# One reciprocal moved ahead of a minimum: sink attention on one Trainium2 core

## What is computed

```python
scores = jnp.einsum('bnqkgd,bnskd->bnkgqs', qb, kb).astype(jnp.float32) * (HEAD_DIM ** -0.5)
...
scores = jnp.where(valid[None, :, None, None], scores, NEG_INF)
sink = sinks.astype(jnp.float32).reshape(N_KV_HEADS, GQA_GROUP)[None, None, :, :, None, None]
sink = jnp.broadcast_to(sink, scores.shape[:-1] + (1,))
probs = jax.nn.softmax(jnp.concatenate([scores, sink], axis=-1), axis=-1)[..., :-1]
out = jnp.einsum('bnkgqs,bnskd->bnqkgd', probs.astype(v.dtype), vb)
```

## Time and profile before

| | |
|---|---|
| median of 3 runs | 1983.57 us (1983.26 to 1983.79) |
| the profiled execution | 1982.3 us |
| its span | 1980.5 us |
| mean granted TensorE clock | 0.996 |
| attention stage, first to last normalisation | 1004.4 to 1111.5 us of the span |

### The profile page before, as it was taken

The page is one execution under the profiler, slowest core; times in us unless marked ns, Lnnn a source line. Parts: engine busy times, 40 slices in busy tenths (PEclk is TensorE's granted clock), DMA queues, the critical chain, the costliest instruction groups (busy, mean ns, idle before and its releaser), DMA issues.

```text
span 1980.5 us, 28829 instructions
## 1 busy us (share of the span) xinstructions
PE 1929.2 (97%) x9242; PEld 1583.7 (80%) x9242; DVE 1431.4 (72%) x2388; ACT 910.5 (46%) x1738; POOL 464.0 (23%) x464
## 2 busy tenths in 40 slices
PE   7899999999999999999999999999999999999998
PEld 7778888888888878888866687788888888888787
DVE  6987777777777786576578748777777777777863
ACT  5654344444444453343268645444444344444531
POOL 3311222222212221010036211222122221212310
PEclk9899999999999999999999999999999999999999
DMA  5333322233333350231000113233332323335201
GB/s 210 107 96 96 95 90 87 79 99 94 102 92 93 109 183 14 67 112 54 0 12 2 59 48 112 81 96 101 95 90 81 95 79 101 95 99 181 98 27 69
DMA packets 214761, 173.29 MB, mean 88 GB/s; under 512 B 8608, under 2 KB 196384, under 8 KB 214688
## 3 DMA queue, kind: packets, MB, share of 16 engines
q1 hardware_dynamic: 213104, 166.60, 26.6%
q10 hardware_dynamic: 1584, 5.77, 0.8%
HBM read 159.75 MB, written 12.58 MB: 87 GB/s over the span
## 4 chain that ended last, share of the span: by engine, by line
PE 86%; DVE 8%; POOL 2%; issue 2%; DMA 1%; ACT 1%; DVEq 0%; ACTq 0%; POOLq 0%
PE ps L787 14%; PE ps L788 14%; PE ps L789 14%; PE ps L295 7%; PE ps L297 7%; PE ps L296 7%; PE ps L884 7%; PE ps L886 7%; PE ps L885 7%; POOL probs L1632 1%; PE ps L356 1%; DVE ps L1597 1%; PE ps L1586 1%; PE ps L1640 1%; PE ps L593 1%
## 5 line engine op out<-in xcount | busy, mean ns | idle before, releaser
L1209 DVE TENSOR_TENSOR H<-H,ps 128x512 f32<-128x512 f32 x496 | 327.9, 685 | 113.0 <-PE ps L886 112.1
L1071 POOL TENSOR_TENSOR s_raw<-s_raw,a_raw 128x512 f32<-128x512 f32 x66 | 87.4, 1326 | 769.2 <-DVE s_lo L1122 660.4
L787 PE MATMUL ps<-t_hi,s_hi 128*128 128x512 f32 x528 | 207.5, 393 | 6.8 <-DVE t_lo L1221 3.8
L788 PE MATMUL ps<-t_lo,s_hi 128*128 128x512 f32 x528 | 206.7, 392 | 0.0
L789 PE MATMUL ps<-t_hi,s_lo 128*128 128x512 f32 x528 | 206.7, 392 | 0.0
L960 ACT ACTIVATE m<-ps 128x512 f32<-128x512 f32 x44 | 26.4, 599 | 265.9 <-PE ps L789 263.5
L788 PE MATMUL ps<-b_lo,a_hi 128*128 128x512 f32 x352 | 137.0, 389 | 0.0
L787 PE MATMUL ps<-b_hi,a_hi 128*128 128x512 f32 x352 | 137.0, 389 | 0.0
L789 PE MATMUL ps<-b_hi,a_lo 128*128 128x512 f32 x352 | 136.9, 389 | 0.0
L885 PE MATMUL ps<-wd_lo,d_ab_hi 128*128 128x512 f32 x336 | 130.7, 389 | 0.0
L884 PE MATMUL ps<-wd_hi,d_ab_hi 128*128 128x512 f32 x336 | 130.7, 389 | 0.0
(11 more groups left out here) (292 smaller groups left out, 5138.9 us busy)
## 6 DMA issues: line engine op xcount, KB each, us to landing
a_raw<-in_w_ff_gate SPq DMA_DIRECT2D x88, 256.0 KB, 2.9
a_raw<-in_w_ff_up SPq DMA_DIRECT2D x88, 256.0 KB, 3.0
s_raw<-in_w_ff_up SPq DMA_DIRECT2D x88, 256.0 KB, 2.9
s_raw<-in_w_ff_gate SPq DMA_DIRECT2D x88, 256.0 KB, 3.0
wd_raw<-in_w_ff_down SPq DMA_DIRECT2D x44, 512.0 KB, 4.3
residual_spill<-H SPq DMA_DIRECT2D x16, 512.0 KB, 2.7
raw<-in_w_ple_gate SPq DMA_DIRECT2D x16, 512.0 KB, 4.9
back<-residual_spill SPq DMA_DIRECT2D x16, 512.0 KB, 5.0
```

The lines of the kernel that those rows point to most:

```text
L787: pe.matmul(ps[:, bank, :], w[0], x[0], start=fresh and k == 0, stop=False, skip_group_check=not fresh)
L788: pe.matmul(ps[:, bank, :], w[0], x[1], start=False, stop=False, skip_group_check=not fresh)
L1071: eng.tensor_tensor(form_raw(name), W_RAW[name][:, :, :], form_raw(other) if other != "A21" else W_RAW["A21"][:, :, :], op).then_inc(summe ...
L1209: dve.tensor_tensor(dst, dst, src, ALU.add).then_inc(F["summed"], 1)
```

## The change

`softmax_max` takes a function that it calls ahead of its fourth head, and the loop hands it the sum and reciprocal of step n+2. So sum and reciprocal n+2 are issued between the third and the fourth minimum of step n+3. Those of step 1 are issued ahead of minimum 2, before the loop, and those of step 31 stay where they were, since there is no minimum left to carry them.

```diff
-        def softmax_max(dve, n):
+        def softmax_max(dve, n, ahead_of_last=None):
...
             for m in range(GQA):
+                if m == GQA - 1 and ahead_of_last:
+                    ahead_of_last()
                 head = banks(2 * par)[:, m * 256:(m + 1) * 256]
...
+            softmax_recip(dve, 1)
             softmax_max(dve, 2)
             for n in range(STEPS_A):
-                if n + 1 < STEPS_A:
+                if n == STEPS_A - 2:
                     softmax_recip(dve, n + 1)
                 probs_copy_even(dve, n)
                 if n + 3 < STEPS_A:
-                    softmax_max(dve, n + 3)
+                    softmax_max(dve, n + 3, lambda: softmax_recip(dve, n + 2))
```

## The result

| | before | changed |
|---|---|---|
| median | 1983.46 us (4 runs, 1983.26 to 1983.79) | 2016.73 us (4 runs, 2014.36 to 2019.46) |
| ratio, 95% interval | | 1.0173 [1.016, 1.0186] |
| the profiled execution | 1982.3 us, span 1980.5 | 2014.36 us, span 2012.5 |

The changed kernel is 33 us slower; 2017 us was forecast.

A forecast was written before the change was run, and what follows sets the result against it. TensorE bounds the kernel (97% busy), but no single engine leads the attention stage. 33.8 - 0.4 + 0.2 = +33.6 us on 1982.3 gives 2015.9; with 1.3 for the median 2017.2, stated as 2017 us, range 2010 to 2024.

The forecast's parts named there:

- The gap is held to the normalisation's end: VectorE's 128x4 addition, now issued under GpSimd's normalisation, waits until that ends: about 1.35 us over its 0.16.
- A closed chain one step long, 4.45 us: Attention stage: exponentials, sum, reciprocal, normalisation, gap's end, next exponentials follow one another, 4.45 us a step.
- 29 steps, +33.8 us: From exponentials 2 to exponentials 31: 95.23 us before, 29 x 4.45 = 129.05 after.
- The ends: Corrections at the first and last attention steps: nothing owed at the start, about 0.4 us given back at the end.
- Far end: Step 31: its sum, no longer kept back by a held w_o_lo, gives back about 0.4 us.
- Near end: Step 1's earlier reciprocal starts normalisation 1 about 1.9 us sooner, near 1009.2; ScalarE's start hides it.
- o_first_lo: GpSimd's 2.35 us instruction behind normalisation 18 outlasts the step's exponentials, so sum 19 waits: +0.2 us.
- The sum: Total over the attention stage: 33.8 - 0.4 + 0.2 = +33.6 us on the profiled execution, giving 2015.9.
- the gap is not held: Rival: the gap slips through beside the normalisation, 3.10 us a step, about 1978 us; chance 0.05.
- for a part only: Rival: GpSimd holds the gap for only part of the normalisation, 1985 to 2009 us; chance 0.05.
- TensorE's clock did not fall: Denies a rival: TensorE, less busy in the attention stage, drops to 1.2 GHz, 2025 to 2068 us; chance 0.05.
- GpSimd did not keep the ports at a hand-over: Denies a rival: behind normalisations 16 and 18 GpSimd's next instruction precedes the gap, 2019 to 2022 us; chance 0.06.

The follow-up runs named there:

- e3_gap_behind_recip: Against the changed kernel, sum and reciprocal go behind all four minima and ahead of the gap, so only the gap moves: 1978.45 us, ratio 0.9978.
- e3b_again: The version with only the gap moved behind the reciprocal, run once more unchanged in a later session: 1979.68 us, ratio 0.9988 to the kernel before.

## Why the prediction was right

- *The gap is held to the normalisation's end.* Right, and by its mechanism: 1.52 us in 29 gaps with a price of 1.35 forecast over 0.16; free with the operand in PSUM, free with GpSimd made to wait, shorter by just what the normalisation is shorter. The rule cited from the Trainium skill (SBUF — State Buffer, "Who interferes with whom") agrees with all four. Its other half, that a VectorE instruction which is first holds GpSimd, the attention stage does not show (with the gap alone behind the reciprocal, the gap is through 0.03 us before the normalisation begins), but the trace before does, in the first layer. A 128x1 addition on GpSimd, whose median is 0.19 us, took 1.18 us behind the start of a VectorE instruction with two SBUF inputs (`H`, `gain`), and ended at 40.62, 0.06 us behind that one's end at 40.56:

```profile
39.28 1.28 DVE L474 SCALAR_TENSOR_TENSOR tmp<-H,small,gain 128x1024 f32<-128x1024 f32 x1 [1.94 <-POOL small L468]
...
39.44 1.18 POOL L337 TENSOR_TENSOR small<-small 128x1 f32<-128x1 f32 x1 [0.19 <-ACT pool_junk L562]
```

- *A closed chain one step long, 4.45 us.* The timeline gives 4.46: exponentials 2.03 (1072.36 to 1074.39), hand-over 0.03, sum to normalisation 0.46, normalisation 1.89, gap's end 0.02, hand-over 0.03.
- *29 steps, +33.8 us.* Exponentials 2 and 31 start at 1009.92 and 1139.34: 129.42 against 95.23, +34.2.
- *The ends.* Far end: from exponentials 31 to normalisation 31 before 1109.56 - 1106.68 = 2.88 us, now 1141.85 - 1139.34 = 2.51; -0.37 against the -0.4 forecast. Near end: normalisation 1 started at 1007.69, and with the 1.53 us of the next point that is 1009.22 in the times of the trace before, where 1009.2 was forecast. `o_first_lo`: the normalisation behind it came 4.52 us after the one before it instead of 4.46, +0.06 where I had put +0.2. Sum 19 started at 1087.81 and ended at 1088.03, 0.02 us behind `o_first_lo`: held, but its own 0.16 us lay within the wait, and I had not taken them off.
- *The sum.* +33.6 was forecast between profiled executions, and the spans differ by 32.0. The missing 1.6 lies outside the stage for the most part: the exponentials of step 2 started 1.53 us earlier, and 1.4 of these stand already at the first product `ps<-t_hi,s_hi` of the first layer's SwiGLU (L787: 95.1 us before, 93.7 here). Between 64 and 70 us TensorE's granted clock was 0.58 in the trace before and 1.00 here (next fence). The streams are the same up to there, so that is no effect of the change. The medians differ by 33.3. That the median came within 0.3 us of 2017 is luck in part: the profiled execution, at 2014.4, lay 1.5 under the 2015.9 forecast for it, and the changed kernel's four executions spread over 5.1 us.
- *Rivals.* That the gap is not held, or for a part only, the 29 gaps of 1.52 us refute. TensorE's clock did not fall: it was 1.00 through the stage, with TensorE busy for 89 of 123 us. The row that I had drawn this rival from says less than I took it for: here TensorE idled for the same 1.39 us at 62.85 us (last fence), and the clock stayed at 1.00. GpSimd did not keep the ports at a hand-over: gaps 17 and 19 took 1.52 us like the others, so both times VectorE got them; in the run with half the normalisation no gap took over 0.67 us, which makes four. Four cases don't make a rule.

The stretch of the earlier trace rows in the changed kernel, and its attention stage; the third figure from the end is the granted clock:

```profile
64.00:70.00 6.00, 6.00 (x55) 6.00 (x55) 4.64 (x6) 2.70 (x5) 0.88 (x1) 1.00 0.01 3
1012.00:1135.00 123.00, 88.88 (x664) 56.50 (x664) 115.01 (x330) 75.89 (x300) 56.33 (x30) 1.00 0.00 1
```

```profile
62.85 0.35 PE L593 MATMUL ps<-band_inner,pool_xn 128*128 128x128 f32 x1 [1.39 <-DVE xt_lo L367]
```

What stays open: the changed kernel's runs spread over 5.1 us and the first four of the kernel before over 0.5. In the later sessions the kernel before spread by 4 to 5 us as well. The clock stretches of the first layer are a candidate. Two traces of one kernel (`e3_gap_behind_recip` and `e3b_again`) show the size: that first product started at 96.7 us in one and 93.6 in the other, and the spans were 1977.7 and 1975.4. Why the clock falls in one execution and not in another, no run shows.

## What to carry to other kernels

Before moving a small VectorE instruction, note which of its operands lie in SBUF and what GpSimd runs at its new place: with two SBUF inputs a 128x4 addition waited for all that was left of a 128x1024 multiplication (1.52 instead of 0.16 us), and because another engine waited for its result, the multiplication's full 1.89 us entered the chain. The cure is to put the small instruction ahead of what starts GpSimd (or 0.1 us behind it), to take one operand from PSUM, or to cut long GpSimd work to the length of its pauses. Here most of what the move was good for, the sum and reciprocal freed from the gap's wait, was to be had by moving the gap alone behind the two, and the rest of the move was not needed: with that the stage ran at TensorE's pace but for one stall.

## What the runs showed that I had not expected

- A wait added on GpSimd, 0.7 us in each step, made the changed kernel 29 us faster.
- The gap and its wait for the last accumulator cost VectorE 0.24 us in its stream, more than the gap's own 0.16: the sum starts 0.65 us behind the fourth minimum with the gap ahead of it, 0.41 without. What needs nothing from the last minimum, like the sum here, can use that time.
- A ScalarE activation of one column (128x1) costs 0.22 us in a row of four, nearly half of the 0.46 us of one of 128x256.
- The holding goes both ways: a 128x1 addition on GpSimd took 1.18 us instead of 0.19 behind a VectorE instruction with two SBUF inputs.
- A GpSimd multiplication of half the columns takes 55% of the time (1.04 against 1.89 us), and a quarter of `o_first_lo` 0.73 us where the whole takes 2.36.
